# Column 5 of x taken as exchanged blocks, small loads issued by GpSimd, a bias table replicated pair by pair, and two VectorE orders in group A

## The reference, cut to what matters

```
h    = rmsnorm(x, g_pre_mix)
proj = h @ w_in + b_in                # aq, ak, av, bq, bk, bv
out_a = sliding-window GQA, learned sinks, shared T5 bucket bias
out_b = chunked attention over own + 8 chunks, clipped relative bias
x = x + rmsnorm(concat(out_a, out_b) @ w_out, g_post_mix)
x = x + rmsnorm(square(relu(rmsnorm(x, g_pre_mlp) @ w_up)) @ w_down, g_post_mlp)
```

## Time and profile before

| | us |
|---|---|
| median of 3 runs (lowest to highest) | 1036.27 (1035.63 to 1036.71) |
| the profiled execution itself | 1036.43 |
| its span in the trace | 1034.6 |
| PE busy in the span | 1025.6 |

### The profile page before, as it was taken

How to read it: one execution, slowest core, us unless ns; L and a number is a source line. 1 busy time by engine, 2 the same in 40 slices (tenths; PEclk the granted TensorE clock), 3 DMA queues, 4 the chain that set the end, 5 groups by cost and what they waited for, 6 DMA issues and landing times.

```text
span 1034.6 us, 15816 instructions
## 1 busy us (share of the span) xinstructions
PE 1025.6 (99%) x5539; PEld 852.6 (82%) x5539; DVE 763.7 (74%) x1499; ACT 470.4 (45%) x987; POOL 212.2 (21%) x201
## 2 busy tenths in 40 slices
PE   9999999999999999999999999999999999999997
PEld 8899877778777888888888888888888888888886
DVE  3854578866679478888988788786444777778997
ACT  5722355554478467846131221221344445444562
POOL 0300000000000003148675675671100000000000
PEclk9999999999999999999999999999999999999999
DMA  9755442110061465135444434446777733454344
GB/s 246 167 148 118 120 129 62 61 53 22 27 201 66 122 171 156 41 132 213 164 173 160 166 132 153 163 140 219 247 241 236 240 98 96 139 195 141 97 139 167
DMA packets 131744, 148.98 MB, mean 144 GB/s; under 512 B 64825, under 2 KB 82113, under 8 KB 129617
## 3 DMA queue, kind: packets, MB, share of 16 engines
q1 hardware_dynamic: 130976, 147.76, 45.8%
q10 hardware_dynamic: 688, 0.20, 0.1%
HBM read 104.70 MB, written 47.49 MB: 147 GB/s over the span
## 4 chain that ended last, share of the span: by engine, by line
PE 96%; issue 2%; DVE 1%; ACT 1%; DVEq 0%; POOL 0%; ACTq 0%; POOLq 0%
PE ps L2199 28%; PE ps L2201 27%; PE ps L2200 27%; PE ps L2412 3%; PE ps L2398 3%; PE ps L2379 2%; PE ps L2323 1%; PE ps L2531 1%; PE ps L2533 1%; PE ps L2519 1%; PE ps L2358 1%; PE ps L2211 1%; PE ps L2549 0%; PE ps L2238 0%; ACT score_a L1151 0%
## 5 line engine op out<-in xcount | busy, mean ns | idle before, releaser
L2200 PE MATMUL ps<-tm_lo,sm_hi 128*128 128x512 f32 (+1 forms) x450 | 174.6, 388 | 0.0
L2201 PE MATMUL ps<-tm_hi,sm_lo 128*128 128x512 f32 (+1 forms) x450 | 174.6, 388 | 0.0
L2199 PE MATMUL ps<-tm_hi,sm_hi 128*128 128x512 f32 (+1 forms) x450 | 174.6, 388 | 0.0
L2199 PE MATMUL ps<-b_hi,wc_hi 128*128 128x512 f32 x448 | 174.6, 390 | 0.0
L2201 PE MATMUL ps<-b_hi,wc_lo 128*128 128x512 f32 x448 | 174.3, 389 | 0.0
L2200 PE MATMUL ps<-b_lo,wc_hi 128*128 128x512 f32 x448 | 174.3, 389 | 0.0
L1457 ACT ACTIVATE sm_hi<-sm_raw 128x512 fp32r<-128x512 f32 x112 | 70.7, 631 | 162.2 <-DMA sm_raw<-u_matrices 162.2
L2103 DVE TENSOR_TENSOR sm_lo<-sm_raw,sm_hi 128x512 fp32r<-128x512 f32 x112 | 77.4, 691 | 78.5 <-ACT sm_hi L1457 77.9
L2199 PEld LDWEIGHTS ps<-tm_hi,sm_hi 128*128 128x128 f32 x450 | 84.5, 188 | 17.6
L2200 PEld LDWEIGHTS ps<-tm_lo,sm_hi 128*128 128x128 f32 x450 | 84.5, 188 | 17.5
L2201 PEld LDWEIGHTS ps<-tm_hi,sm_lo 128*128 128x128 f32 x450 | 84.5, 188 | 17.2
(11 more groups left out here) (244 smaller groups left out, 2053.7 us busy)
## 6 DMA issues: line engine op xcount, KB each, us to landing
u_matrices<-stage SPq DMA_DIRECT2D x112, 256.0 KB, 2.0
sm_raw<-u_matrices SPq DMA_DIRECT2D x112, 256.0 KB, 2.6
up_raw<-in_w_up SPq DMA_DIRECT2D x16, 1024.0 KB, 4.9
w<-in_w_down SPq DMA_DIRECT2D x64, 256.0 KB, 3.9
w_raw<-in_w_in SPq DMA_DIRECT2D x8, 512.0 KB, 3.5
xr<-in_x SPq DMA_DIRECT2D x8, 512.0 KB, 4.6
x_rows<-xr SPq DMA_DIRECT2D x8, 512.0 KB, 4.6
xf<-x_rows SPq DMA_DIRECT2D x8, 512.0 KB, 3.6
```

The source lines that it names most:

```text
L2199: pe.matmul(out, w_hi_, x_hi_, start=start, stop=False)
L2200: pe.matmul(out, w_hi_, x_lo_, start=False, stop=False)
L2201: return pe.matmul(out, w_lo_, x_hi_, start=False, stop=stop)
```

## The change

`EXCHANGED` gets column 5 as well. Its eight transposing matmuls go; four block DMAs and one more VectorE transpose come. The row form of columns 5 to 7, still needed for the sums of squares, is loaded by two DMAs of 1536 B rows into `x_rows` in place of three of 512 B rows. The squares are placed later, five over columns 0 to 4 (640 elements) and then over the rest (384 elements). All twelve small loads move from SP to GpSimd, count on one semaphore and are waited for by one wait of VectorE (after `first_lo(6)`) and one of GpSimd (ahead of `arow`). The value weights' first parts are split after column 7. Four `rcols` instead of two are made on ScalarE. The table of group A is replicated in four DMAs, two heads each, with the bias loads in between. In group A `turn_a(4)` comes before the split of step 11, and at step 14 the first of two `tile_scaled` comes before the split.

```diff
-SQUARED = ((), (), (0, 1, 2, 3), (4, 5, 6, 7), (8, 9), (10, 11, 12), (13, 14, 15), ())
+SQUARED = ((), (), (), (0, 1, 2, 3, 4), (5, 6, 7), (8, 9, 10, 11, 12), (13, 14, 15), ())
-EXCHANGED = (6, 7)
-SPLIT_WITH = ((), (1,), (2,), (3,), (4,), (5, 6), (7,), ())
+EXCHANGED = (5, 6, 7)
+KX = KT - len(EXCHANGED)
+SPLIT_WITH = ((), (1,), (2,), (3,), (4, 5), (6, 7), (), ())
...
+            def load_x_rows(h):
+                half = slice(h * (T // 2), (h + 1) * (T // 2))
+                sp.dma_start(x_rows[:, half].rearrange("p t k n -> p t (k n)"),
+                             x[:, KX * P:KT * P].rearrange("(t p) n -> p t n", p=P)[:, half]).then_inc(s_in[KX + h], 16)
+            def replicate_pair(p):
+                sp.dma_start(a_rep[p::4], bass.AP(bdram.tensor, p * (LA + LB), [[4 * (LA + LB), 2], [0, P], [1, LA]])
+                             ).then_inc(s_rep, 16)
...
-            for k in range(4, KT):
-                load_x(k)
-            sp.dma_start(relrow[:, 0:513], rel).then_inc(s_tab, 16)
-            sp.dma_start(t5row[:], t5).then_inc(s_tab, 16)
-            load_values(0)
+            load_x(4)
+            load_x_blocks(5)
+            for h in range(2):
+                load_x_rows(h)
+            sp.wait_ge(s_xhi, 1)
+            sp.wait_ge(s_xlo, 1)
             load_x_blocks(6)
             sp.wait_ge(s_xt, 2)
             sp.wait_ge(s_sq, 1)
             load_x_blocks(7)
-            for k in range(1, 5):
+            for k in range(5):
                 load_values(k)
-            sp.dma_start(g2, g_pre_mlp).then_inc(s_const, 16)
-            sp.dma_start(sink, bass.AP(sinks.tensor, 0, [[0, P], [1, 8]])).then_inc(s_const, 16)
...
             sp.wait_ge(s_bv, 1)
-            sp.dma_start(bv_cols[:, 0:5], b_in[:, AV:AV + 5]).then_inc(s_bv, 16)
+            for g in range(4):
+                sp.dma_start(vrow[:, 32 * g:32 * g + 32], bv_rows[32 * g:32 * g + 5]).then_inc(s_bv, 16)
+            sp.wait_ge(s_rows, 2)
+            sp.dma_start(bdram[:, 0:LA], arow[:]).then_inc(s_rowst, 16)
+            sp.dma_start(bdram[:, LA:LA + LB], brow[:]).then_inc(s_rowst, 16)
...
-            sp.dma_start(a_rep, bass.AP(bdram.tensor, 0, [[LA + LB, 8], [0, P], [1, LA]])).then_inc(s_rep, 16)
+            replicate_pair(0)
+            sp.wait_ge(s_bv, 65)
             sp.dma_start(bv[:], bass.AP(vrow.tensor, 0, [[0, P], [1, VW]])).then_inc(s_bv, 16)
+            for p in range(2):
+                sp.wait_ge(s_rep, 16 * (p + 1))
+                load_bias(p)
+                replicate_pair(p + 1)
             load_fill(0)
+            sp.wait_ge(s_rep, 48)
+            replicate_pair(3)
...
+            pool.wait_ge(s_xt, 2)
+            pool.dma_start(relrow[:, 0:513], rel).then_inc(s_const, 16)
+            pool.dma_start(t5row[:], t5).then_inc(s_const, 16)
+            pool.wait_ge(s_id, 4)
+            pool.dma_start(bv_cols[:, 0:5], b_in[:, AV:AV + 5]).then_inc(s_const, 16)
+            pool.dma_start(g2, g_pre_mlp).then_inc(s_const, 16)
...
+            pool.wait_ge(s_const, 192)
             for lo, hi, b in t5_runs():
...
+                if k == 5:
+                    dve.wait_ge(s_const, 192)
+                    nc.vector.transpose(bv_rows[:], bv_cols[:]).then_inc(s_bv, 1)
+                    nc.vector.tensor_scalar(bcol[:, 1:9], bcol[:, 1:9], -SCALE, None, ALU.mult).then_inc(s_bsc, 1)
+                    nc.vector.tensor_scalar(sink, sink, -1.0, None, ALU.mult).then_inc(s_sink, 1)
...
-                    for t in range(T - 2):
+                    for t in range(T // 2):
                         last = nc.vector.tensor_scalar(rcols[:, t * P:(t + 1) * P], ones[:], rs1[:, t:t + 1], None, ALU.mult)
...
                 normalize_a(n)
+                if n == LATE_TILE:
+                    take(halves_done(n - 1)[:1])
                 splits(n)
                 if n == LATE_TILE:
-                    take(halves_done(n - 1))
+                    take(halves_done(n - 1)[1:])
...
-                splits(n + 1)
                 if n in TURNED_LAST:
                     turn_a(TURNED_LAST[n])
+                splits(n + 1)
```

More of the change, by code:

```diff
@@ L299, in build @@
         bv = sb("bv", 204, [P, VW])
-        xraw = sb("xraw", 168, [P, KT, T, P])
+        xraw = sb("xraw", 168, [P, KX, T, P])
+        x_rows = sb("x_rows", 188, [P, T, KT - KX, P])
         w1_raw = sb("w1_raw", 64, [P, KT, FIRST_TILES * P])
@@ L311, in build @@
                          for n, dt in (("wv_raw", F32), ("wv_lo", F32R)))
-        x_blocks = {k: sb(f"x_blocks{k}", at, [P, SEQ]) for k, at in zip(EXCHANGED, (76, 108))}
-        x_turned = {k: sb(f"x_turned{k}", at, [P, SEQ]) for k, at in zip(EXCHANGED, (112, 76))}
+        x_blocks = {k: sb(f"x_blocks{k}", at, [P, SEQ]) for k, at in zip(EXCHANGED, (92, 76, 108))}
+        x_turned = {k: sb(f"x_turned{k}", at, [P, SEQ]) for k, at in zip(EXCHANGED, (112, 116, 76))}
         bv_cols = sb("bv_cols", 121, [P, 32])
@@ L503, in build @@
         s_g1 = sem("g1_landed")
[L504 removed]
+        s_tab = sem("value_halves_landed")
         s_rows = sem("bias_rows_ready")
         s_rowst = sem("bias_rows_stored")
[L507 removed]
+        s_bv = sem("value_biases_turned_stored_then_landed")
         s_rep = sem("bias_rows_replicated")
@@ L786, in _ @@
             load_bias(2)
+            sp.wait_ge(s_rep, 64)
             load_bias(3)
@@ L811, in _ @@
             replicate_bias(7)
-            sp.wait_ge(s_rep, 16 + 16 * 8)
+            sp.wait_ge(s_rep, 64 + 16 * 8)
             load_bias(4)
@@ L963, in _ @@
                                     pattern=[[-1, P]], channel_multiplier=1).then_inc(s_id, 1)
-            nc.gpsimd.memset(bv_cols[:], 0.0).then_inc(s_bv, 1)
-            pool.wait_ge(s_tab, 32)
+            nc.gpsimd.memset(bv_cols[:], 0.0).then_inc(s_id, 1)
+            pool.wait_ge(s_xt, 2)
[4 more added lines that the diff above has]
+            pool.dma_start(g2, g_pre_mlp).then_inc(s_const, 16)
+            pool.dma_start(sink, bass.AP(sinks.tensor, 0, [[0, P], [1, 8]])).then_inc(s_const, 16)
+            for b in range(2):
+                pool.dma_start(bcol[0:64, 1 + 2 * b:3 + 2 * b], b_in[64 * b:64 * b + 64, 0:2]).then_inc(s_const, 16)
+                pool.dma_start(bcol[64:128, 1 + 2 * b:3 + 2 * b], b_in[64 * b:64 * b + 64, 2:4]).then_inc(s_const, 16)
+            pool.dma_start(bcol[:, 13:15], b_in[:, AK:AK + 2]).then_inc(s_const, 16)
+            pool.dma_start(bcol[:, 5:9], b_in[:, 10:14]).then_inc(s_const, 16)
+            pool.dma_start(bcol[:, 9:13], b_in[:, 14:18]).then_inc(s_const, 16)
+            pool.wait_ge(s_const, 192)
             for lo, hi, b in t5_runs():
@@ L1065, in square_rows @@
             def square_rows(n):
-                first, t = n // T * KH, n % T
-                if t == 0:
-                    for k in range(first, first + KH):
+                t = n % T
+                if n == 0:
+                    for k in range(KX):
                         act.wait_ge(s_in[k], 16)
                     act.wait_ge(s_x0, 16)
+                elif n >= T and t % (T // 2) == 0:
+                    act.wait_ge(s_in[KX + t // (T // 2)], 16)
                 if n >= 2:
                     act.wait_ge(s_sq, n - 1)
-                nc.scalar.activation(sq[:, n % 2], xraw[:, first:first + KH, t], ACT.Square,
-                                     accum_out=(ya1 if first else ss1)[:, t:t + 1]).then_inc(s_sq, 1)
+                if n < T:
+                    nc.scalar.activation(sq[:, n % 2], xraw[:, :, t], ACT.Square, accum_out=ss1[:, t:t + 1]).then_inc(s_sq, 1)
+                else:
+                    nc.scalar.activation(sq[:, n % 2, 0:KT - KX], x_rows[:, t], ACT.Square, accum_out=ya1[:, t:t + 1]
+                                         ).then_inc(s_sq, 1)
             def value_hi(k):
@@ L1106, in _ @@
                     act.wait_ge(s_ch1, 1 + STEP)
-                    for t in range(T - 2, T):
+                    for t in range(T // 2, T):
                         last = nc.scalar.activation(rcols[:, t * P:(t + 1) * P], ones[:], ACT.Copy, scale=rs1[:, t:t + 1])
                     last.then_inc(s_rcol, 1)
-                if k >= 5:
-                    value_hi(k - 5)
             def tile_hi(i):
@@ L1121, in tile_hi @@
                                      bias=bias_of(e)).then_inc(s_ehi, 1)
-            value_hi(3)
-            value_hi(4)
+            for k in range(2):
+                value_hi(k)
             act.wait_ge(s_rowp, 1)
             nc.scalar.activation(rrow[:], two(6), ACT.Copy).then_inc(s_row, 1)
+            for k in range(2, 5):
+                value_hi(k)
             act.wait_ge(s_bsc, 1)
@@ L1543, in _ @@
                 elif k == KT - 1:
-                    for n in range(3):
+                    for n in range(5):
                         value_lo(n)
[L1546 to L1552, removed]
             def tile_scaled(i):
@@ L1594, in _ @@
                     tile_scaled(i + 2)
-            dve.wait_ge(s_bv, 98)
```

(1 more changed line is left out.)

28 lines of the change are left out of this document (6 added, 22 removed).

## The result

The changed kernel takes 1055.53 us (median of 4 runs, 1053.85 to 1056.52), the kernel before on the same chip 1036.49 (1035.63 to 1036.83). The ratio is 1.0184, with a 95% interval of 1.0172 to 1.0197. The forecast of 1035.0 is 20.5 us off, and on the wrong side.

What follows compares the result with a forecast made beforehand. PE bounds the kernel, busy 1025.6 of 1034.6 us. Gains of 0.62 (front) and 0.65 (group A) make 1.27; 1036.43 - 1.27 = 1035.16, less 0.16 gives 1035.0 us, with 8 in 10 between 1034.0 and 1036.6.

Steps and rivals of the forecast that it cites:

- Bias table pair by pair: Group A's table replication: smaller pieces make replication and `bv` come earlier; PE waits for neither, so nothing gained or lost.
- the last of my signs of being wrong: Anywhere on PE: a wait elsewhere that takes back the 1.3 us would show the prediction wrong.
- Transposes of column 5: Front: taking eight transposes off PE gains 0.87 us if VectorE, ScalarE and the DMAs meet PE's needed times.
- Column 4 and the squares: Front: rows land at 18.8, five squares run on ScalarE to 22.9, 0.1 late; cost nothing, cover 1.0 us.
- Column 6: Front, the tight place: blocks land at 30.4; a PE wait of 0.25 us leaves a gain of 0.62.
- L: Front: landing of column 6's blocks, forecast 30.4, best 29.7, worst 31.6; `rcols` allows 30.5 to 30.8.
- SP's issuing is not what decides: Front, column 6: eight block DMAs issue in 8.37 us, the last near 25, landing at 28.3, before the transfers' 30.4.
- column 6's blocks late: Front rival, chance 0.22: blocks at 31.6 or more, 0.1 gained to 0.5 lost, time 1035.5 to 1036.2.
- Small loads by GpSimd: Front: twelve loads at 1 to 1.5 us each, landed by 27.5, before VectorE's wait near 32.1; cost nothing.
- Group A and the sum: Group A: `turn_a(4)` before the split gains 0.65 us, PE restarting at 132.6; added to the front's gain.
- 0.62 and 0.65: Gains in us forecast for the front (0.87 less a 0.25 wait) and for group A's new order.
- forecast 1.27 us: Whole kernel: total gain, front 0.62 plus group A 0.65.

Runs made afterwards that it cites:

- experiment 1: Changed kernel with each two-head replication walking the 128 copies in its outermost dimension: 1037.98 us, ratio 1.0010.
- experiment 2: Changed kernel with one replication of all eight rows and the bias loads behind it, as in the kernel before: 1035.77 us, ratio 0.9997.
- 4: Kernel before with only its one replication exchanged for the changed kernel's four pairs, waits and bias loads: 1059.05 us, ratio 1.0219.
- 9: Changed kernel, pair by pair with the same waits, each pair as two one-row DMAs with copies outermost: 1036.45 us, ratio 0.9999.
- 3: Changed kernel with the four pair replications issued back to back without waits, bias loads behind the fourth: 1056.82 us, ratio 1.0201.
- 10: Changed kernel with two replications of four rows, rows outermost, issued back to back, bias loads then as before: 1041.74 us, ratio 1.0049.
- 8: Changed kernel with one eight-row replication and both of group A's former orders, so the front's change alone: 1036.38 us, ratio 1.0002.
- 7: Kernel before with group A's two new VectorE orders alone: 1035.95 us, ratio 0.9992.
- 12: Changed kernel with one eight-row replication, row loads of columns 5 to 7 issued behind column 6's blocks: 1035.75 us, ratio 0.9995.
- 5: Changed kernel with one replication of all eight rows, copies outermost, both bias loads behind it: 1036.77 us, ratio 1.0006.
- 6: Changed kernel with one eight-row replication, copies outermost, and two of five squares moved behind column 4's high part: 1037.44 us, ratio 1.0007.
- Experiment 11: Changed kernel with one eight-row replication, row loads of columns 5 to 7 issued ahead of column 5's blocks: 1036.93 us, ratio 1.0003.

## Why the prediction was wrong, step by step

*Bias table pair by pair: "Nothing".* This is the step that failed, with all of the loss. I had read PE's waits, found neither the replication nor `bv` among them, and concluded that smaller pieces come earlier. I gave no duration to a pair. The trace of before had a warning: while the one DMA of 1.5 MB ran alone, the DMA view shows 4 to 5 tenths of the engines busy, about half of them, eight, for eight rows. I should have asked what a pair takes, and what stands behind its wait in SP's queue, as I did for the small loads. Where I had put nothing, the runs show a stop of PE of 15.6 us and 2.6 us more for the lower clock behind it. Experiments 1, 2 and 4 show that it is the pairs, 1 and 9 that it is the order of the dimensions, 3 that it is not the waits, 10 the price per row. A pair takes 10 us, nearly as long as all eight rows, so four in a row take 40 us instead of 11.4. Why the first exchange then had to be late is SP's order: it stands behind the last bias load. No rival had this case; only the last of my signs of being wrong, a wait elsewhere on PE, covers it.

*Transposes of column 5.* The eight matmuls went, as forecast.

*Column 4 and the squares: "cost nothing".* The squares cost what I said (0.72 each, 19.92 to 23.53 in experiment 2), the landing did not: 19.9 to 20.6 instead of 18.8. I took its 5.2 us to landing from before; issued at 13.84, it needed 6.7 in the changed kernel. Price 0 to 0.7 us of PE.

*Column 6.* This was the tight place and I called it so, but L was 31.66 in the changed kernel, 31.11 in experiment 2, 32.19 in 8 and 30.71 in 10, all with the same front, against my 30.4. From L to column 7's products it took 8.96 us in the first three; my 8.3 to 8.6 and the transposes of 0.87 make 9.2 to 9.5. The error is in "SP's issuing is not what decides". Four block DMAs took 5.5 to 6.9 us to issue behind a full queue, not the 4.2 from the earlier trace rows, the row loads went out from 20.5 to 21.7, and in experiment 2 the queue had nearly run empty by then (24 GB/s or less from 20.0 to 20.7 us). Column 7 started from 0.5 us earlier to 0.55 later than before, not 0.62 earlier. Of my rivals "column 6's blocks late" describes it.

*Small loads by GpSimd.* Right that they cost nothing, and the issues were at the lower bound: 0.56 us each, not 1 to 1.5. The last landed 4.3 us after its issue had ended, at 17.8; I had taken 3.1. SP, rid of them, issues the first replication 2.6 us earlier (42.16 against 44.76).

*Group A and the sum.* In the changed kernel itself the delay covers this step. In experiment 2 the split near 131 starts 14.53 us after `wf_hi`, which waits for `w_raw` to land (116.95), as it started 14.52 us after it before (116.91): the turning saved and the `tile_scaled` moved ahead cancel, and PE restarts when the split ends, at 132.84 instead of 133.30. I had said 132.6. The row of PE:

```profile
132.84 0.47 PE L2220 MATMUL ps<-x_hi,wf_hi 128*128 128x512 f32 x1 [0.79 <-DVE wf_lo L1728]
```

But PE was there 0.8 us early, having saved its time in the front and at 119, and waited. Both gains pay for the same restart, which in this trace hangs on a landing and not on PE. So 0.62 and 0.65 do not add: together they brought 0.46 there. In experiments 7, 9 and 12, with `wf_hi` at 115.39, 116.74 and 116.12, there was no stop near 133, and the spans are 1034.1, 1034.1 and 1033.8. But experiment 2, with its stop, has 1034.1 too, and in 5 and 8, with `wf_hi` at 117.05 and 116.58, PE came later from the front (column 7's products at 40.88 and 41.15, against 40.07 in 2) and did not stop either. What the landing alone is worth is not shown; no run moved it by itself.

Of the forecast 1.27 us, then, little is left: the spans of experiments 1, 2, 5 to 9 and 12 lie between 0.8 us below and 0.5 above that of the kernel before, and their times differ from its by less than their intervals can tell, but for experiment 1, which is 0.1% slower. Experiment 11 is left out here for its slow profiled execution; its ratio of 1.0003 is no different from 1.

## What to carry to other kernels

When a DMA is cut into parts, work out what each part takes before asking who waits for it: look at which dimension is outermost and at the DMA share while it runs. With a replication, put the copies outermost. Before adding a wait to a queue, read what is issued behind it; here a wait for a bias table held back an exchange that had nothing to do with it. And two savings ahead of one restart that hangs on a transfer are not a sum.

## What was not expected of the hardware

With the rows outermost, the bias load behind a replication of two rows goes out after 10 us, behind one of eight rows after 11.4 (12.5 in experiment 2), behind two of four rows after 19.6 and behind four of two rows, in flight together, after 33.7: DMAs with few rows outermost, issued together, kept no more engines busy than one of them. By the shares and rates of experiments 3 and 10 one such engine moved 25 GB/s in pieces of 1536 B; with eight rows in the kernel before it was some 20 (151 to 190 GB/s over eight). With the copies outermost, the eight rows took 8.4 us and a quarter of their bytes 4.5 to 5.5, with other loads beside both. And a stop of 15.6 us cost PE another 2.6 us after it: a granted clock of 0.50, the level of 1.2 GHz, from 94.17 to about 100.
